# A two-block hybrid network on one core: the cell's steps behind each load's block products, and two pieces of VectorE work dealt out differently

## The reference

```python
ada = c_act @ w_ada[l] + b_ada[l]
shift, scale, gate = jnp.split(ada, 3, axis=-1)
h = rmsnorm(x, norm_g[l]) * (1.0 + scale[:, None, :]) + shift[:, None, :]
p = h @ w_in[l]
mq, mk, mv, mo, mz, mi, mf, rq, rk, rv, rz = split_cols_2(p)
...
cell = mlstm_chunkwise(mq_c, mk_c, mv, mi + b_igate[l], mf + b_fgate[l])
y_m = jax.nn.sigmoid(mo) * head_layernorm(cell, gn_m[l], N_HEADS_MLSTM) * jax.nn.silu(mz)
...
ret = retention_chunkwise(rq_h, rk_h, rv)
y_r = head_layernorm(ret, gn_r[l], N_HEADS_RET) * jax.nn.silu(rz)
y = jnp.concatenate([y_m, y_r], axis=-1) @ w_out[l]
x = x + gate[:, None, :] * y
```

## Time and profile before

| | |
|---|---|
| median of 3 runs | 3738.32 us (3737.96 to 3744.14) |
| profiled execution, its own time | 3736.55 us |
| its span | 3734.7 us |
| PE busy | 3459.2 us (93%) |
| DVE, ACT, POOL busy | 40%, 21%, 39% |
| granted PE clock over the execution | 0.942 of full speed |
| chain that ended last, PE's share | 84% |
| cell stage, layer 0 (products to turn 3 of the last head) | about 2301 to 2931 us |
| cell stage, layer 1 | about 3028 to 3631 us |

### The profile page before, as it was taken

One profiled execution on the slowest core, in us unless ns is written; L12 is line 12 of the kernel. 1 busy time (PEld: TensorE's weight loads), 2 busy tenths in 40 slices (PEclk: granted clock), 3 DMA queues, 4 the chain that ended last, 5 costly groups with the idle time before them and its releaser, 6 DMA issues.

```text
span 3734.7 us, 37648 instructions
## 1 busy us (share of the span) xinstructions
PE 3459.2 (93%) x13991; PEld 2316.4 (62%) x13991; DVE 1482.7 (40%) x2529; ACT 782.3 (21%) x1349; POOL 1442.5 (39%) x1372
## 2 busy tenths in 40 slices
PE   6999978999999999987899998999999989999998
PEld 5665554666666556443554444887897458889953
DVE  5121438753344231235753224355554233344321
ACT  2211313222111031222221111223211013321110
POOL 0008989900000000899100002767563047776600
PEclk6999987999999999978899998999999999999999
DMA  5111000002232111111004331222222222222211
GB/s 185 45 34 34 29 23 23 1 12 89 92 94 89 52 51 45 40 34 34 1 18 124 124 100 57 75 95 91 91 94 87 58 68 68 68 68 69 79 43 47
DMA packets 259174, 236.41 MB, mean 63 GB/s; under 512 B 20870, under 2 KB 257202, under 8 KB 258996
## 3 DMA queue, kind: packets, MB, share of 16 engines
q1 hardware_dynamic: 258996, 234.02, 20.5%
HBM read 231.90 MB, written 2.10 MB: 63 GB/s over the span
## 4 chain that ended last, share of the span: by engine, by line
PE 84%; DVE 9%; POOL 3%; ACT 2%; issue 1%; DMA 0%; DVEq 0%; ACTq 0%; SPq 0%; POOLq 0%
PE ps L396 34%; PE ps L880 20%; PE ps L426 10%; PE ps L634 3%; PE ps L660 3%; DVE arena L1397 3%; DVE arena L1401 2%; PE ps L930 2%; DVE arena L1403 2%; PE ps L646 2%; PE ps L574 2%; ACT arena L1025 1%; PE ps L412 1%; PE ps L974 1%; PE ps L504 1%
## 5 line engine op out<-in xcount | busy, mean ns | idle before, releaser
L396 PE MATMUL ps<-hT,wring 128*128 128x512 f32 (+1 forms) x1568 | 577.5, 528 | 2.5 <-ACT arena L1025 2.5
L396 PE MATMUL ps<-arena,wring 128*128 128x512 f32 (+1 forms) x1280 | 493.5, 544 | 10.6 <-DVE arena L1397 10.6
L396 PEld LDWEIGHTS ps<-hT,wring 128*128 128x128 f32 x1568 | 301.1, 193 | 266.5 <-issue 248.1
L1921 POOL TENSOR_TENSOR arena<-wring 128x512 f32<-128x512 f32 x72 | 93.5, 1298 | 950.4 <-DMA wring<-in_w_in 642.7
L1885 POOL TENSOR_TENSOR arena<-arena,posi 128x512 f32<-128x512 f32 (+1 forms) x360 | 413.5, 1149 | 30.0
L426 PE MATMUL ps<-hT,wring 128*128 128x512 f32 (+1 forms) x1088 | 417.0, 537 | 0.0
L396 PEld LDWEIGHTS ps<-arena,wring 128*128 128x128 f32 x1280 | 243.3, 192 | 247.6 <-issue 228.2
L1397 DVE TENSOR_TENSOR arena<-arena 128x768 f32<-128x768 f32 (+7 forms) x141 | 185.6, 1316 | 382.1 <-ACT arena L1025 378.6
L426 PEld LDWEIGHTS ps<-hT,wring 128*128 128x128 f32 x1088 | 206.0, 194 | 183.2 <-issue 174.0
L1025 ACT ACT_TABLE_LOAD x148 | 189.9, 1283 | 509.7 <-PE ps L504 113.3
L1025 ACT ACTIVATE arena<-ps 128x256 f32<-128x256 f32 (+6 forms) x307 | 135.8, 442 | 695.5 <-PE ps L396 305.7
(11 more groups left out here) (175 smaller groups left out, 4710.0 us busy)
## 6 DMA issues: line engine op xcount, KB each, us to landing
wring<-in_w_in SPq DMA_DIRECT2D x128, 1024.0 KB, 5.3
wring<-in_w_mod SPq DMA_DIRECT2D x24, 1024.0 KB, 7.9
wring<-in_w_out SPq DMA_DIRECT2D x24, 1024.0 KB, 5.5
wring<-in_w_ada SPq DMA_DIRECT2D x24, 1024.0 KB, 5.1
wring<-in_w_conv_out SPq DMA_DIRECT2D x8, 512.0 KB, 3.5
wring<-in_w_gla_out SPq DMA_DIRECT2D x8, 512.0 KB, 4.0
wring<-in_w_attn_out SPq DMA_DIRECT2D x8, 512.0 KB, 4.0
arena<-in_x SPq DMA_DIRECT2D x1, 2048.0 KB, 9.8
```

Of the source, the lines that this page charges most:

```text
L396: last = eng.matmul(o_(out), a, b_, start=(i == 0), stop=(i == len(parts) - 1))
L1921: pool.link(eng.tensor_tensor(t1, w[:, 0:4, P:2 * P], w[:, 0:4, 0:P], ALU.subtract))
```

## The change

It has three parts.

1. `steps2()` takes the projection's element first and the core's second. Between products and corners of a load there is now the step "scores" (with "turn"), and between corners and the next products the step "values". Before, it was the other way round. In the tail the "out" products come first too.
2. DVE's modulation sums become a generator. "mod load" only sets it up, and after each of the steps products, scores, turn and values two of the eight instructions are taken from it; the step "mod" takes what is left.
3. The gate rows: ACT's Abs, Exp and Ln follow its copy in the first products step of the layer. DVE's first three instructions (`gate_scans`) follow corners (0, 0), the other five (`gate_rows`) corners (0, 1).

```diff
-            for part in (b, a):
+            for part in (a, b):
...
-                fn(rM[0:4, :], rF[0:4, :], ACT.Abs)
-                fn(rM[0:4, :], rM[0:4, :], ACT.Exp, scale=-1.0)
-                fn(rM[0:4, :], rM[0:4, :], ACT.Ln, ("f ln", l), bias=1.0)
...
                         fn(U1, bank_of["left", k][:, 0:HALF], ACT.Copy, ("u1", k))
+                        if (n, x[0]) == (0, 0):
+                            act.stage("cell_gates")
+                            fn(rM[0:4, :], rF[0:4, :], ACT.Abs)
+                            fn(rM[0:4, :], rM[0:4, :], ACT.Exp, scale=-1.0)
+                            fn(rM[0:4, :], rM[0:4, :], ACT.Ln, ("f ln", l), bias=1.0)
+                            act.stage("cell")
...
             def modulate(L, g):
+                for _ in mod_by_product(L, g):
+                    pass
+
+            def mod_by_product(L, g):
...
+                    yield
                     for k in range(1, KD):
+                        dve.stage("modulation")
                         stt(sums, w[:, k, :], cT[:, col0 + 8 * c + k:col0 + 8 * c + k + 1], sums, M_, A_,
                             ("mod summed", L, g) if (c, k) == (ncol - 1, KD - 1) else None)
+                        yield
...
+                def gate_scans():
+                    dve.stage("cell_gates")
+                    eng.wait_ge(*at(("f ln", l)))
+                    eng.wait_ge(*at(("free", ("if", l))))
+                    stt(rF[R, :], rF[R, :], 0.0, rM[R, :], ALU.min, S_)
+                    dve.link(eng.tensor_tensor_scan(rM[R, :], rF[R, :], rI[R, :], 0.0, A_, ALU.max))
+                    dve.link(eng.tensor_tensor_scan(rB[R, :], gscan[R, 0:TX], rF[R, :], 0.0, M_, A_))
+                    dve.stage("cell")
+
+                def gate_rows():
...
                     if kind == "mod load":
                         if l < DEPTH - 1:
-                            dve.stage("modulation")
-                            modulate(L + 1, x[0])
-                            dve.stage("cell")
+                            summing = mod_by_product(L + 1, x[0])
+                    elif kind == "mod":
+                        for _ in summing:
+                            pass
+                        dve.stage("cell")
...
+                    if kind in ("products", "scores", "turn", "values"):
+                        for _ in range(2):
+                            next(summing, None)
+                        dve.stage("cell")
+                    if (kind, n) == ("corners", 0):
+                        if x[0] == 0:
+                            gate_scans()
+                        elif x[0] == 1:
+                            gate_rows()
```

More of the change, by code:

```diff
@@ L1723, in _ @@
                 tt(hsum[3], quarter[0][1], hsum[1], S_, ("h sums", l))
-                dve.stage("cell_gates")
                 R = slice(0, 4)
                 v3 = lambda x_: x_[R, :].rearrange("p (a b) -> p a b", b=CH)
-                eng.wait_ge(*at(("f ln", l)))
-                eng.wait_ge(*at(("free", ("if", l))))
-                stt(rF[R, :], rF[R, :], 0.0, rM[R, :], ALU.min, S_)
-                dve.link(eng.tensor_tensor_scan(rM[R, :], rF[R, :], rI[R, :], 0.0, A_, ALU.max))
-                dve.link(eng.tensor_tensor_scan(rB[R, :], gscan[R, 0:TX], rF[R, :], 0.0, M_, A_))
-                tt(rU[R, :], rB[R, :], rM[R, :], S_)
-                tt(rW[R, :], rI[R, :], rB[R, :], S_)
-                cp(small[R, 33:36], rM[R, CH - 1:TX - 1:CH])
-                tt(v3(rI), v3(rU), small[R, 32:36].unsqueeze(2).broadcast_to([4, NCH, CH]), A_)
-                tt(v3(rF), v3(rW), rU[R, CH - 1:TX:CH].unsqueeze(2).broadcast_to([4, NCH, CH]), A_, ("gate rows", l))
+                def gate_scans():
[7 more added lines that the diff above has]
+                def gate_rows():
+                    dve.stage("cell_gates")
+                    tt(rU[R, :], rB[R, :], rM[R, :], S_)
+                    tt(rW[R, :], rI[R, :], rB[R, :], S_)
+                    cp(small[R, 33:36], rM[R, CH - 1:TX - 1:CH])
+                    tt(v3(rI), v3(rU), small[R, 32:36].unsqueeze(2).broadcast_to([4, NCH, CH]), A_)
+                    tt(v3(rF), v3(rW), rU[R, CH - 1:TX:CH].unsqueeze(2).broadcast_to([4, NCH, CH]), A_, ("gate rows", l))
+                    dve.stage("cell")
                 dve.stage("cell")
@@ L1778, in finish @@
                     ts(HN, src[:, 0:HD2], small[:, 54:55], small[:, 57:58], S_, M_, ("hn", k))
+                summing = iter(())
                 for kind, n, *x in steps2():
```

## The result

| | before | after |
|---|---|---|
| median (range) | 3741.23 us (3737.96 to 3747.92, 4 runs) | 3782.83 us (3777.83 to 3785.53, 4 runs) |
| ratio to before, with 95% interval | | 1.0107 (1.0088 to 1.0127) |
| profiled execution, its own time | 3736.55 us | 3785.53 us |
| its span | 3734.7 us | 3783.6 us |
| first cell stage | 638.0 us | 665.1 us |

The change makes the kernel slower by 41.6 us; the forecast said +41 and 3779. A stage is counted from its first L412 matmul (the gates' projection) to the first L988 matmul (the output). The two cells together are 45.5 us longer. By the window view PE's idle time in them grew by 19.0 and 9.9 us (41.6 to 60.6, 27.1 to 37.0); the other 8.1 and 8.5 us are busy time for the same number of matmuls, the slow clock. The stages between and behind them have the same length to 0.7 us.

A forecast was written before the change was run, and what follows sets the result against it. PE, busy 93% of the span, bounds the kernel, so its waits and clock count. Gains of 73.0 us against costs of 66, 10, 34 and 4 give +41, 3779 us; 8 in 10 range 3752 to 3803 us.

The forecast's parts named there:

- Sum: Whole kernel: gains of 73 against costs of 66, 10, 34 and 4 give +41 us, 3779 us; chance 0.70.
- Starts: Start of each layer: first corners' waits for U2, 5.44 and up to 5.7 us, go, with 2.9 slow clock each.
- what is late next: Layer starts: after gate work moves, the products' own end is late next; moved gate rows cost 0.5 us a layer.
- Cost 1: Core ends beside a retention projection, eight places: the last turn loses its cover; 46.0 us idle plus 20 clock, 66.
- Cost 2: Heads 1 to 3, layer 1: turn 3 waits since NI follows ACT's Sigmoid, table load and silu; 10 us (4 to 14).
- Cost 3: Heads 1 to 3, layer 0: dealt out sums beside busy POOL delay mod_finish, turn 3 and U2; 34 us.
- Cost 4: Tail: first "out" waits for turn 3's result, values 1 loses cover, 1.5 us a layer; with gate rows 4 us.
- Full price: Rival, both cells: every sum is blocked and tables cost their drain; +59 to +70 us, 3802 us; chance 0.12.
- Cheap sums: Rival: sum pairs slip between POOL's instructions, short gaps lower the clock little; +6 to +15, 3748 us; chance 0.11.
- Faster: Rival: eight core ends are as short as the tail's 2.46 us and cost no clock; -28, 3710 us; chance 0.07.

The follow-up runs named there:

- mixed order: Changed kernel with the old order from the fourth core on, the new order only beside the first three; 3740.41 us, or 3734.26 with modulation sums in one row.
- mixed order with all parts: Changed kernel, old order from the fourth core on, with dealt out sums and moved gate rows kept: 3740.41 us, 0.9997 of the kernel before.
- without the root: Changed kernel with the variance's square root left out in cores 3 to 7 of each cell, so no table load there: 3771.76 us, ratio 1.0079.

## Why the prediction was right, point by point

- **Sum.** Forecast +41, medians +41.6. By layers its terms give +22 and +19; measured +27.1 and +18.4. The total is nearer than its terms, whose errors cancel, so that it is met to 1 us is luck; the place and the kind of the loss are not. By kind its terms hold at most 8.5 us more of slow clock (20 + 2.7 + 7.5 - 21.7); measured were 16.6.
- **Starts** (-15.9: 5.44 and 5.7 idle, 2.9 clock each, 0.5 back each). The waits went, but the cells gain 2.9 and 5.4, 8.3 in all, 8.2 by the medians. The step that failed is "what is late next": it is ACT's u1 behind a `silu` that waits for POOL's taps, 3.0 us and 1.7 to 1.8 of slow clock a layer. The forecast gave the moved gate rows "a fraction of a us"; they held up POOL by 3.4 us a layer. That PE's waits would go without this delay is inferred from the chain above; no run has the gate rows where POOL is quiet. And 1.8 us of slow clock a layer, taken as gone, stayed behind the gates' matmuls.
- **Cost 1** (66, of it 46.0 idle). The place, the count, the order of events on ACT and the size of a gap are shown by the trace and by three kernels. Idle was 41.3: the plain gap is 4.54, the 4.5 of the working without contention; DVE's last instruction took 0.41 us (3552.86 at the end of core 5), so the 0.5 added for POOL was not there. Core 3 took 6.77 and 7.46 for 7.7. The clock cost 1.2 to 1.9 a place where products follow, and not 2.5. In the first cell L966 adds 5.0 us (1.84, 1.57, 1.58) where 0.6 was taken for ACT's modulation. Net of what the old order pays in the same places and in the tail it is 48.5 us by the profiles, 42.4 by the medians. That the table load is 1.28 of each gap and no more is shown: it left with 1.3. The Trainium skill ("ScalarE: Activation LUTs", What ACT_TABLE_LOAD costs) adds 1.38 us of drain to each load. The trace has none here: at 3191.07 a load stands 0.03 us behind a Silu, and the next function starts 0.01 us behind the load.
- **Cost 2** (10). Not there: the turns of heads 1 to 3 wait 1.38 or 1.39 us at full clock, less than the 1.64 of the earlier trace rows. The turn comes 9.5 us behind D (3189.42 to 3198.90), near the low end's 9.2 without contention. The waits of first scores that went were worth a little less than forecast: the kernels with the mixed order have 17.3 to 17.9 us idle in the second cell, those with the old order and new gate rows 22.9 and 22.1, so 5 us; by length (600.9 to 604.1 against 605.2 and 607.5) it is 1 to 7 us. The terms say 7.
- **Cost 3** (34). The mixed order with all parts has a first cell 6.4 us longer than the gate rows alone; the terms there (34 less 21.3 for the modulation waits and 12.0 for the first scores) say +1. The wait at `mod_finish` was 2.36, 2.35 and 1.30, not 4.5; the turn did not wait; the bank's 3.47 was not foreseen. In the first groups of these heads the eight sums took 8.5, 8.5 and 7.4 us, where the working has 10.3 beside POOL and the idle rate of the earlier trace rows gives 4.1. The first pair took up to 2.8 us, later ones 1.3 to 2.2. PE's waits in these heads come to 20.9 us and the slow clock behind the bank's wait to 7.1, together 28 where 34 was taken.
- **Cost 4** (4). The wait of "out" is 0.98 us in each layer, against 0.8 and 1.4 before; the L930 row behind it is 14.05 us long for 12.25. But that row stands right behind core 6's wait of 4.54 us, so its 1.8 us of slow clock belong to cost 1. Of its own this cost has at most 0.2 us a layer; the tail did not lose cover, its turns wait as before.
- **Rivals.** "Full price" is out: no drain, and the first groups' sums took 0.93 to 1.06 us each, not 1.26. "Cheap sums" is not refuted by the eight gaps, which with their clock come near its 54; against it stand the time, and the eight sums, which took about twice their idle time. "Faster" rested on ends as short as the tail's; they are 4.5 us, and even without the root 3.1 to 3.3.
- What the prediction did not have at all is how the parts act on each other. It priced the sums in the new order only. Added to the new order (with its gate rows) the dealt out sums give 3782.8 - 3800.8 = -18.0, added alone they give +16.3. Gate rows are worth about the same on either order, -7.2 (3808.0 to 3800.8) and -8.2.

What stays open: in the profiled executions the first cell of the mixed order is 641 to 642 us long with sums in a row, dealt out, or with "mod" one load later, with similar idle time in heads 1 to 3 under three different waits. That it hangs on the sums being there is shown (moved away, these waits are gone); whether it is DVE's time or its place in ACT's order was not taken apart.

## What to carry to other kernels

When two lists of unequal length are interleaved, look at where the shorter one ends: there the longer one's last steps lose their cover, and an order that costs little along the rest of the list costs a full round trip through the other engines at that point (here 6.2 us for each of six places). Move that one step behind the next piece of independent work, or keep the old order just there. Splitting a long row of instructions into pieces ends the blocking of others but puts its own end behind every wait in between; ask who needs the last piece, and when. Before moving DVE work beside POOL's, ask what waits for POOL: here both became slower.

## What the runs showed of the hardware

- A wait of 4.40 us was followed by matmuls at the lower clock level (granted clock 0.76 over the next 7 us), one of 3.07 us at the same place by none (1.00). But another of 3.07 us was followed by 1.7 us of slow clock: at 3.1 to 3.3 us these traces have both.
- DVE's gate scan over 4x512 elements took 2.20 us beside POOL's pair sums (2320.03 in the profile after), 1.21 before. The pair sums beside it took 2.06 us for 1.26: both engines are held up, and four partitions are enough for it.
- A table load took 1.28 us in each chain shown here, and its removal shortened the wait by the same.
